# A hybrid S5 and sparse-attention decoder layer on one Trainium2 core: the SSM branch, the key selection and the adaLN sums move inside the attention loop

## What is computed

```
mod = silu(c) @ w_ada + b_ada              # 6 vectors of 1024: sh1 sc1 g1 sh2 sc2 g2
hn  = rmsnorm(x)*(1+sc1)+sh1;  proj = hn @ w_in       # u q k v qi ki wi
y_ssm  = S5(u): B, a diagonal complex scan of 64 states in 32 groups, C, D,
         gelu, then y * sigmoid(y @ w_glu + b_glu)
y_attn = for each query: index scores = sum_h wi_h * relu(qi_h . ki), the top 128
         causal keys kept, softmax attention of 8 heads of 64 over those keys
h   = x + g1 * (concat(rmsnorm(y_ssm), rmsnorm(y_attn)) @ w_out)
hn2 = rmsnorm(h)*(1+sc2)+sh2;  up = causal conv of width 3 over (hn2 @ w_up)   # 5632 columns
out = h + g2 * ((gelu(gate)*val) @ w_down)
```

## Time and profile before

| what | us |
|---|---|
| median of 3 runs | 926.57 |
| lowest, highest | 920.92, 931.33 |
| profiled execution: span from first to last instruction | 939.8 |
| TensorE busy, share of span | 774.1 (82%) |
| VectorE busy | 530.9 (56%) |
| ScalarE busy | 292.0 (31%) |
| GpSimd busy | 324.9 (35%) |
| mean granted TensorE clock | 0.845 of 2.4 GHz |

### The profile page before, as it was taken

One profiled execution on the slowest core, in us unless ns is written; L12 is line 12 of the kernel. 1 busy time (PEld: TensorE's weight loads), 2 busy tenths in 40 slices (PEclk: granted clock), 3 DMA queues, 4 the chain that ended last, 5 costly groups with the idle time before them and its releaser, 6 DMA issues.

```text
span 939.8 us, 9759 instructions
## 1 busy us (share of the span) xinstructions
PE 774.1 (82%) x3436; PEld 612.8 (65%) x3436; DVE 530.9 (56%) x948; ACT 292.0 (31%) x426; POOL 324.9 (35%) x161
## 2 busy tenths in 40 slices
PE   0239888897617498899859879999999999799997
PEld 0237676676405276667548767888888888688886
DVE  4989945589899947221778169465555555400002
ACT  5121122532322133135342223334344443311111
POOL 1902277241295500000013414343334444144440
PEclk9659999689755658557779979999999999999999
DMA  8737221112300400350752612223332222222212
GB/s 272 252 118 228 90 94 42 46 45 90 90 0 1 50 1 17 35 180 0 257 191 88 225 46 64 71 89 97 108 107 89 89 89 89 89 90 89 89 45 90
DMA packets 68227, 90.33 MB, mean 96 GB/s; under 512 B 11723, under 2 KB 45283, under 8 KB 68068
## 3 DMA queue, kind: packets, MB, share of 16 engines
q1 hardware_dynamic: 68195, 89.93, 30.6%
HBM read 85.23 MB, written 4.69 MB: 96 GB/s over the span
## 4 chain that ended last, share of the span: by engine, by line
PE 59%; DVE 31%; issue 4%; ACT 4%; POOL 1%; SPq 1%; DMA 0%; ACTq 0%; DVEq 0%; POOLq 0%
PE bank L1386 15%; PE bank L1387 15%; PE bank L1388 15%; DVE arena L968 7%; PE bank L1391 4%; PE bank L1541 2%; DVE arena L1074 2%; PE bank L1634 2%; PE bank L1559 2%; DVE arena L1124 2%; DVE stat L1121 1%; DVE arena L1070 1%; PE bank L1631 1%; DVE arena L966 1%; DVE arena L1077 1%
## 5 line engine op out<-in xcount | busy, mean ns | idle before, releaser
L457 POOL TENSOR_TENSOR w_lo<-w_raw,w_hi 128x2048 fp32r<-128x2048 f32 (+1 forms) x49 | 224.1, 4575 | 504.2 <-ACT w_hi L590 341.2
L1386 PE MATMUL bank<-act_hi,w_hi 128*128 128x512 f32 (+1 forms) x424 | 168.5, 397 | 5.7 <-issue 3.2
L1388 PE MATMUL bank<-act_hi,w_lo 128*128 128x512 f32 (+1 forms) x424 | 169.4, 399 | 0.0
L1387 PE MATMUL bank<-act_lo,w_hi 128*128 128x512 f32 (+1 forms) x424 | 168.9, 398 | 0.0
L1391 PE MATMUL bank<-ident,arena 128*128 128x128 f32 (+1 forms) x220 | 48.7, 361 | 67.8 <-ACT arena L768 29.9
L590 ACT ACTIVATE w_hi<-w_raw 128x2048 fp32r<-128x2048 f32 (+1 forms) x27 | 50.4, 1867 | 159.1 <-PE bank L1388 129.1
L1386 PEld LDWEIGHTS bank<-act_hi,w_hi 128*128 128x128 f32 (+1 forms) x424 | 80.9, 191 | 25.5 <-issue 7.0
L1391 PEld LDWEIGHTS bank<-ident,arena 128*128 128x128 f32 (+1 forms) x220 | 33.9, 185 | 94.4 <-issue 41.2
L1387 PEld LDWEIGHTS bank<-act_lo,w_hi 128*128 128x128 f32 (+1 forms) x424 | 81.0, 191 | 19.2 <-issue 0.8
L1388 PEld LDWEIGHTS bank<-act_hi,w_lo 128*128 128x128 f32 (+1 forms) x424 | 80.7, 190 | 17.4 <-issue 0.8
L968 DVE SCALAR_TENSOR_TENSOR arena<-arena,c_col 128x512 f32<-128x512 f32 x77 | 80.1, 1040 | 2.7
(11 more groups left out here) (267 smaller groups left out, 1228.9 us busy)
## 6 DMA issues: line engine op xcount, KB each, us to landing
arena<-in_w_ada SPq DMA_DIRECT2D x12, 2048.0 KB, 12.0
w_raw<-in_w_up SPq DMA_DIRECT2D x44, 512.0 KB, 4.7
w_raw<-in_w_down SPq DMA_DIRECT2D x22, 512.0 KB, 4.0
w_raw<-in_w_in SPq DMA_DIRECT2D x10, 1024.0 KB, 5.3
w_raw<-in_w_out SPq DMA_DIRECT2D x4, 1024.0 KB, 5.6
xh<-in_x SPq DMA_DIRECT2D x4, 512.0 KB, 5.0
s_mem<-lag_dram SPq DMA_DIRECT2D x16, 128.0 KB, 5.5
arena<-in_x SPq DMA_DIRECT2D x4, 512.0 KB, 5.2
```

The costliest lines, as they stand in the source:

```text
L457: nc.gpsimd.tensor_tensor(w_lo[:, slot, 0:width], w_raw[:, slot, 0:width], w_hi[:, slot, 0:width].bitcast(F32), ALU.subtract).then_inc(S[" ...
L1386: T.matmul(dst, lhs_hi, rhs_hi, start=start, stop=False)
L1387: T.matmul(dst, lhs_hi, rhs_lo, start=False, stop=False)
L1388: return T.matmul(dst, lhs_lo, rhs_hi, start=False, stop=stop)
```

## The change

It touches every stretch up to the MLP loop:

- Start: all four w_ada chunks are summed on VectorE, but for 2 of the 8 k of chunk 3 (`ADA_DVE`), which TensorE multiplies directly; the rope tables and S5 parameters move behind them. The small loads go to ScalarE's queue, so that SP issues x, w_ada and w_in one after another. ScalarE writes `act_hi` itself.
- `first_project` takes the k of the activations one by one, as each is transposed and split. The order of the units becomes qi, k, q, u, v; `tail` comes after qi with tiles of its own.
- `w_lo` of the units 0 to 9, and of the out and first up units but one, is made on VectorE (`lo`); GpSimd gets most of the S5 parameters (`s5_rest`, `turn_step`, `s5_diagonals`, `source_of_v` of half 1, `weigh_lags`).
- The index scores are made in pairs of heads, one on array rows 0 to 63 and one on rows 64 to 127 (`score_pair`), between the tiles of the q and u projections; relu and sum work in four banks. All rounds of `top_k`, one tile at a time (`ROUNDS`), go into attention, a tile of keys ahead of its use.
- Attention: logits go in twos. Half of the v projection, all of S5 by step 14, gelu, the GLU product, the squares and four of the w_ada sums are placed at steps of it.
- Between: out projection in 512-column token rows (activations stationary); h stays in token rows; norm and modulation use transposes after it; the first up iteration works on tiles 0 to 2 first (384 columns) and on tile 3 apart (128 columns): 192 matmuls in place of 96.
- MLP: the gate2 sums move into the up iterations 1 to 6. `down` has the activations stationary and 512 columns of w_down moving, and writes token rows: the 32 transposes go, and each half row of a tile is stored when it is done.

The core of the diff:

```
-S5_AT = {2: ("V", 0, 0), 3: ("V", 0, 1), 4: ("u", 0, 0), 5: ("states", 0, 0), 7: ("lags", 0, 0), 11: ("y", 0, 0),
-         12: ("V", 1, 0), 13: ("V", 1, 1), 14: ("u", 1, 0), 16: ("states", 1, 0), 17: ("lags", 1, 0), 21: ("y", 1, 0),
-         27: ("x", 0, 0), 28: ("x", 1, 0), 29: ("x", 2, 0), 30: ("x", 3, 0)}
+S5_AT = {0: ("values", 2, 0), 1: ("values", 3, 0), 2: ("V", 0, 0), 3: ("V", 0, 1), 4: ("V", 1, 0), 5: ("V", 1, 1),
+         6: ("u", 0, 0), 7: ("states", 0, 0), 8: ("lags", 0, 0), 9: ("u", 1, 0), 10: ("states", 1, 0), 11: ("lags", 1, 0),
+         12: ("y", 0, 0), 14: ("y", 1, 0), 17: ("g", 0, 0), 20: ("g", 1, 0),
+         21: ("glu", 0, 0), 22: ("glu", 1, 0), 23: ("glu", 2, 0), 24: ("glu", 3, 0)}
+GELU_AT = {16: 0, 19: 1}
+ADA_STEPS = {n: 4 for n in range(24, 32)}
+ROUNDS = {**{i: 2 for i in (*range(10), *range(13, 24))}, 10: 3, 11: 0, 12: 3}
...
+            def score_pair(pair):
...
+                T.matmul(a, qi_hi[up, g, ts], ki_hi[up, ks], start=True, stop=False)
+                T.matmul(b, qi_hi[down, g, ts], ki_hi[down, ks], start=True, stop=False)
+                T.matmul(a, qi_hi[up, g, ts], ki_lo[up, ks], start=False, stop=False)
+                T.matmul(b, qi_hi[down, g, ts], ki_lo[down, ks], start=False, stop=False)
...
-            for i in range(ATT_UNITS + 2):
-                if i < ATT_UNITS:
-                    logits(i)
-                if 1 <= i <= ATT_UNITS:
-                    turn_probs(i - 1)
-                if i >= 2:
-                    values(i - 2)
-                if i in S5_AT:
-                    s5(*S5_AT[i])
+            for i in range(0, ATT_UNITS + 4, 2):
+                if i < ATT_UNITS:
+                    logits(i)
+                    logits(i + 1)
+                for j in (i - 2, i - 1):
+                    if j in S5_AT:
+                        s5(*S5_AT[j])
+                    if 0 <= j < ATT_UNITS:
+                        turn_probs(j)
+                    if 0 <= j - 1 < ATT_UNITS:
+                        values(j - 1)
...
+            def down(slot, k0, first):
+                wh, wl = down_weights(slot)
+                for i in range(2):
+                    for t in (2, 3, 0, 1) if first else range(TT):
+                        ts = slice(t * P, (t + 1) * P)
+                        fh, fl = ff_hi[:, k0 + i, ts], ff_lo[:, k0 + i, ts]
+                        for nb in range(2):
+                            ns = slice(512 * nb, 512 * nb + 512)
+                            ins = mm3(bank[2 * t + nb][:], fh, fl, wh[:, i, ns], wl[:, i, ns], first and i == 0, False)
```

More of the change, by code:

```diff
@@ new lines, in _ @@
+            s5_rest()
+            for n in (1, 2, 4, 8):
+                turn_step(n)
+            s5_diagonals()
+            future(1)
+            turn_step(16)
+            future(2)
+            turn_step(32)
+            future(3)
+            pool.wait_ge(S["turn_ready"], 1)
+            pool.wait_ge(S["vt_ready"], 1)
+            for part in range(3):
+                source_of_v(G, link, 1, part)
+            pool.wait_ge(S["rot_ready"], 9)
+            pool.wait_ge(S["turned_ready"], 13)
@@ L1117, in top_k @@
-            def top_k(tiles, first=0, last=TOPK // 8):
-                dve.wait_ge(S["future_set"], tiles[-1])
-                for _ in range(first, last):
+            def top_k(rounds, ending):
+                for tiles in rounds:
+                    dve.wait_ge(S["future_set"], tiles[-1])
                     after = [marked(V.max(top8[t % 2], score[t])) for t in tiles]
@@ L1346, in _ @@
-            later_ada(6, 8)
-            with dve.Fori(0, UPS) as j:
+            ada_at = [0]
+            for i in range(0, ATT_UNITS, 2):
+                logits(i)
+                logits(i + 1)
+                if i in (HEADS + 2, 2 * HEADS + 2, 3 * HEADS + 2):
+                    heads_out(i // HEADS - 1)
+                for j in (i, i + 1):
+                    top_k(*top_k_rounds(j))
+                    for back in (1, 2):
+                        stage, half, part = S5_AT.get(j - back, ("none", 0, 0))
+                        if stage == "lags" and back == 1:
+                            add_d(half)
+                        elif stage == "states" and back == 1:
+                            for step in range(3):
+                                scan(half, step)
+                        elif stage == "g" and back == 1:
+                            g_lo(2 * half)
+                            g_lo(2 * half + 1)
+                        elif stage == "glu" and back == 2:
+                            gated(half)
+                    for _ in range(ADA_STEPS.get(j, 0)):
+                        late_ada(ada_at[0] // KD, ada_at[0] % KD, ada_at[0] % KD + 1)
+                        ada_at[0] += 1
@@ L1350, in _, with convolved @@
+            for k in range(KD):
+                hn_lo(k, slice(0, 3 * P), k)
+                if k == 1:
+                    rstd_of_h((3,))
+            for k in range(KD):
+                hn_lo(k, slice(3 * P, SEQ), KD + k)
+            gate2_at = [0]
+            def convolved(j, steps):
                 for q in range(4):
@@ L1711, in _ @@
-            for t in range(TT):
-                ins = T.matmul(bank[6][:, t * P:(t + 1) * P], ones[:], rstd_diag[:, t], start=True, stop=True)
-            ins.then_inc(S["rstd_spread"], 1)
-            def up(j, first):
+                    logits(i + 1)
+                for j in (i - 2, i - 1):
[5 more added lines that the diff above has]
+                        values(j - 1)
@@ L1745, in up @@
                             ins.then_inc(S["up_mm"], 1)
[L1747 removed]
+            up_first()
+            with pe.Fori(1, GATE2_SUM) as j:
+                up(j)
             pe.wait_ge(S["ada_used"], 8)
             for i in range(2):
[L1751 removed]
+                ins = T.matmul(bank[6 + i][:], ones[:], gate2_acc[i], start=True, stop=True)
             ins.then_inc(S["ada_sum_ready"], 1)
[L1753 to L1754 removed]
```

1641 lines of the change are left out of this document (935 added, 706 removed).

## The result

The kernel after takes 800.13 us, median of 4 runs (799.23 to 804.29), beside 928.95 us for the kernel before on the same chip (920.92 to 944.42): a ratio of 0.864, 95% interval 0.858 to 0.870. The forecast was 782 us, range 752 to 832. The profiled execution after has a span of 797.4 us; before it was 939.8. The four executions of after lie within 0.6%.

A forecast was written before the change was run, and what follows sets the result against it. Bound by waits in the first half, TensorE in the second. Terms -16-57-31-45+8-8 = -149 us took the span from 939.8 to 791; 1.4% off gave 780, plus 2 for anything missed 782, range 752 to 832.

The forecast's parts named there:

- Start: Up to the first modulated tile: 61.4 us becomes 45, with w_ada steps on VectorE; saved 16, range 11 to 18.
- Projections: First modulated tile to first logits: 193.8 us becomes 137, TensorE 125 plus 12 for hand-offs; range 126 to 160.
- The rival of a VectorE bound: In the projections GpSimd's S5 work holds VectorE: its 111 us becomes 139, the stretch 165, total 810; chance 0.13.
- the 6.2 us: Projections: the 12 score pairs with full overlap of the row halves; 12.4 us without overlap, 8 taken.
- Attention: Attention stretch: 190.8 us becomes 160, range 145 to 190; VectorE and TensorE level in steps 16 to 31.
- one wait of about 10 us for the lag loads before y(1): Attention: sign of a right forecast, TensorE waiting once, about 10 us, for S5's half 1 lags to be loaded.
- S5's round trips, the second rival: Attention: y(1), gelu 0 and gelu 1 each stop TensorE by 13 us; attention 190, total 812; chance 0.13.
- Between: Between attention and the first up product: 106.9 us becomes 62, range 55 to 78; saved 45.
- first up product: First up iteration, split into 384 and 128 columns: 27.6 us becomes 36, range 30 to 46; lost 8.
- Up, down, end: MLP loops and end: sums cost 1 us, down's 5.2 idle leaves 1, end 9.7 becomes 4.7; together -8.
- slower, 0.02: Up to the first up product's end the clock stays low, about 870 matmuls costing 0.20 us more: 956; chance 0.02.
- From span to median: Whole kernel: profiled execution before lay 1.4% above its median, so a span of 791 us became 780 for runs.

The follow-up runs named there:

- the run with the filler at its right place: Kernel after, with matmuls that compute nothing placed in TensorE's idle times before the logits of steps 12 and 14 and before y(1); median 803.03 us.
- the rescheduled run: Kernel after, with VectorE's top-k rounds and late w_ada sums moved into its idle times and GpSimd's two w_lo held back; median 792.34 us.

## Why the prediction was right, and where it was off

**Start** (45, measured 42.3). Right: VectorE's sums began at 16.5 and each step took 0.78 us; the load kept up. The w_lo took 2.29, and the sums over partitions lay beside it instead of ahead of it.

**Projections** (137, measured 132.7). Two errors offset each other. TensorE's work was forecast at 125 us, and first to last matmul is 129.5 with one gap of 0.24: the pairs took 8.6 us for 8 and the transposes 0.105 each for 0.114, but the 456 matmuls of 512 columns took 0.248 us on the mean and not 0.230, because one right behind a transpose or a pair costs some 0.1 more and the first twelve were 0.43 apart. The 12 us for hand-offs were too much: 3.2 are left, ahead of the first matmul and behind the last. The rival of a VectorE bound is out here: VectorE was busy 106.7 us (forecast 111), its operations lost 2.1 us in all against the shortest of their kind, and where the two engines met it was mostly GpSimd that waited. While VectorE's w_lo of 2.29 us ran, an operation of 16 columns on GpSimd took 2.33:

```profile
127.82 2.29 DVE L1113 TENSOR_TENSOR w_lo<-w_raw,w_hi 128x2048 fp32r<-128x2048 f32 x1
```
```profile
127.86 2.33 POOL L540 TENSOR_TENSOR arena<-arena 128x16 f32<-128x16 f32 x1
```

The Trainium skill (SBUF — State Buffer, SBUF: two separate sides) says that the port is an exclusive lock. This row and the experiment without lag weights agree, and so do the operations that the prediction took as free of it: MAX8 and MATCH_REPLACE8 keep their times beside GpSimd (0.55 and 0.54 us at 203 to 205, as at 228).

The Trainium skill (TensorE: Matmul & The Clock Gate, Part 3: Packing small matmuls) says that matmuls on different row groups run at the same time. The traces bear that out, in whatever order the halves are issued. They don't bear out the 6.2 us that the prediction made of it: each pair has about 0.2 us on top of its three matmul times (0.88 against 3 x 0.230), 2.4 us for 12 pairs.

**Attention** (160, measured 170.2). This is the step that failed. By its parts: steps 0 to 7 27.3 for 32; 8 to 15 56.1 for 46; then 46.6 for 36 and 40.2 for 36. The forecast's VectorE work was right: 53.9 us less the 8.9 of waiting for GpSimd's instructions is 45.0, for 46. The term that was missing is the lock in attention. I had priced it for the projections only, though the earlier trace rows showed it, and the two-input operations ahead of the scan, the copy and the lag additions are open to it. So is a scan: in the first profile of before and in that of after none lay beside GpSimd, but in the run with the filler at its right place one of 1.20 us took 3.12, beside GpSimd's L516:

```profile
212.00 3.12 DVE L1366 TENSOR_TENSOR_SCAN s_mem<-arena 128x512 f32<-128x512 f32 x1
```

The "one wait of about 10 us for the lag loads before y(1)" was there, at 5.5 us, and behind step 16's logits, so it belongs to the 46.6. The last part is no level race of two engines, as the sum had it: 9 us of its 40.2 were the late sums', most of it by the clock, as leaving them out shows; the rescheduled run, with 20 of the 32 sum steps still there, took 31.3. Of the 46.6 before it TensorE was idle 11.3, of which the wait for the lag loads, 5.5, is the largest piece.

S5's round trips, the second rival: TensorE waited 5.5 us for lag loads and 2.4 before the glu product, far from the 25 named as its sign.

**Between** (62, measured 64.2) and **first up product** (36, measured 35.4) came out near their sums, the second with some luck: its 384-column matmuls took 20.0 us for 17, the first of them at the low clock, the 128-column ones 12.4 for 11 (0.11 us apart, for the 0.114 assumed), and of the 4 us of feed and conv almost nothing showed. One lock is there as well, 4.5 us on an operation of one column; TensorE felt 0.4 of it.

**Up, down, end** (351.3, measured 352.6). Gate2's idle time at the start of down is gone wholly (5.2 us, not 4.2), and the end took 3.8. But each matmul takes 0.2324 us in up and 0.2333 in down for 0.2289, over 1488 matmuls 5.7 us, for which the forecast had no term ("for which I have no term"). The up stretch hides its part: before's 223.5 us held some 970 matmuls, the first of down among them, and a start partly at the low clock, and after's 224.2 hold 960.

**Clock** (slower, 0.02). Projections ran at 1.00 by the table; the rows add that the first twelve matmuls, up to 50 us, were 0.43 apart, at the low clock. Whether transposes count for the clock is still not told apart; the filler shows that work in an idle stretch held it at 1.00 where it had fallen to 0.50.

**From span to median.** The forecast took 1.4% off the span, because before's profiled execution lay that much above its median. After's does not: its time of 799.23 is 0.1% below its median. (An execution is 1.8 to 2.0 us longer than its span in both kernels, 799.23 for 797.4 and 944.48 for 942.5, which the forecast left out.) A span of 791 without that step would have made 794; the step is 11 of the 18 us of error and the largest single term.

## What to carry to other kernels

Where a change moves GpSimd's work, lay its timeline against VectorE's two-input operations and copies in every stage that it reaches, not only where most of it went; a single block can sit on the one small operation that a transfer waits for. Spread background work of an engine in small pieces between the steps that another engine waits on: in steps 24 to 31 the sums cost 9 us as 32 steps, four in each, and nothing that shows as 20, mostly two in each. The wait of 2.0 us there was followed by 17 us of TensorE at the low clock, so look behind a short wait too. And do not carry the offset between a profiled execution and its median over to another kernel.

## What the runs showed that I had not expected

- Matmuls on the two row halves started in pairs even when the program had three of one half ahead of the other (139.15 and 139.16 us, for the first and the fourth).
- The lock works both ways: six GpSimd operations of a few columns took 2.25 to 2.41 us beside VectorE's w_lo in the projections.
- The up loop's matmuls, unchanged in the code, are 0.2289 us apart in both profiles of before and 0.2324 in after (0.2333 in its last iterations and in down), at a granted clock of 1.00 in all. It is not VectorE's added sums, which are over by the last iterations. Why is open; no run tells it.
- A gain of 2 to 5 us in attention was often not seen at the end. In the run with the w_lo held back the next stage ran at clock 0.93 for 0.98 and was 2.8 us longer.
